# Rotary half-swap moved from DMAs to TensorE, and compression weights moved into the streaming weight ring, in a two-layer decoder trunk

## The reference, cut to what matters

```python
def apply_rope(x, cos, sin):
    half = HEAD_DIM // 2
    x1, x2 = xf[..., :half], xf[..., half:]
    return jnp.concatenate([x1 * cos - x2 * sin, x2 * cos + x1 * sin], axis=-1)

def compress_blocks(k, w1, w2, pe):            # 63 blocks of 32 tokens, stride 16
    flat = (k[:, idx] + pe).reshape(B, nc, N_KV, CMP_L * HEAD_DIM)
    return jax.nn.silu(flat @ w1) @ w2         # w1: 2048 x 256

q = apply_rope(q, cos, sin)                    # 8 heads of 64
kc, k_s, k_w = (apply_rope(t, cos, sin) for t in (kc, k_s, k_w))
y_attn = nsa_mixer(q, kc, vc, k_s, v_s, k_w, v_w, nsa_g, cmp_k_w1, ...)
```

## Time and profile before

| | us |
|---|---|
| median of three executions | 3422.77 |
| the profiled execution | 3423.22 |
| its span, first to last instruction | 3421.5 |
| PE busy | 3256.8 (95%) |
| POOL busy | 1281.6 (37%) |
| DVE busy | 1588.4 (46%) |
| mean granted TensorE clock, share of full speed | 0.977 |

### The profile page before, as it was taken

How to read it: one execution, slowest core, us unless ns; L and a number is a source line. 1 busy time by engine, 2 the same in 40 slices (tenths; PEclk the granted TensorE clock), 3 DMA queues, 4 the chain that set the end, 5 groups by cost and what they waited for, 6 DMA issues and landing times.

```text
span 3421.5 us, 38488 instructions
## 1 busy us (share of the span) xinstructions
PE 3256.8 (95%) x15485; PEld 2654.5 (78%) x15485; DVE 1588.4 (46%) x1998; ACT 771.8 (23%) x1274; POOL 1281.6 (37%) x1271
## 2 busy tenths in 40 slices
PE   5999998998999999999999999989979999999999
PEld 4888886676778888888878888867658788888887
DVE  6643245887537443232365333568754432222223
ACT  2100114666212000000010001256651210000002
POOL 2433332333434444444424334223334344444442
PEclk7999999999899999999999999999999999999999
DMA  6434620000512221111133355200014111111111
GB/s 228 134 102 135 189 77 25 1 1 1 197 43 87 74 69 55 50 50 50 50 125 99 111 160 153 50 13 1 1 64 153 38 49 50 50 50 50 50 45 61
DMA packets 281881, 255.66 MB, mean 75 GB/s; under 512 B 10091, under 2 KB 262247, under 8 KB 281192
## 3 DMA queue, kind: packets, MB, share of 16 engines
q1 hardware_dynamic: 266866, 199.27, 19.7%
q10 hardware_dynamic: 14838, 53.94, 4.1%
HBM read 215.42 MB, written 30.41 MB: 72 GB/s over the span
## 4 chain that ended last, share of the span: by engine, by line
PE 88%; DVE 7%; ACT 2%; issue 2%; POOL 0%; ACTq 0%; POOLq 0%; DVEq 0%
PE lin L917 76%; PE aux L1093 2%; DVE pTL L1637 2%; PE pv L1107 2%; DVE negm L1631 1%; PE pv L1108 1%; PE lin L1069 1%; PE lin L1070 1%; PE pv L957 1%; PE lin L1048 1%; ACT pTH L1340 1%; DVE acc L711 1%; ACT prob L1324 0%; DVE tmp L1657 0%; PE lin L1072 0%
## 5 line engine op out<-in xcount | busy, mean ns | idle before, releaser
L890 POOL TENSOR_SCALAR whi<-wraw 128x512 fp32r<-128x512 f32 x476 | 386.5, 812 | 1589.6 <-PE lin L917 1565.8
L917 PE MATMUL lin<-hH,whi 128*128 128x512 f32 x2272 | 708.0, 393 | 15.4 <-DVE hL L521 12.6
L892 POOL TENSOR_TENSOR wlo<-wraw,whi 128x512 fp32r<-128x512 f32 x476 | 706.9, 1485 | 39.7
L917 PE MATMUL lin<-hL,whi 128*128 128x512 f32 x2272 | 703.4, 391 | 0.0
L917 PE MATMUL lin<-hH,wlo 128*128 128x512 f32 x2272 | 702.2, 390 | 0.0
L917 PEld LDWEIGHTS lin<-hH,whi 128*128 128x128 f32 x2272 | 425.1, 189 | 107.7 <-issue 22.0
L917 PEld LDWEIGHTS lin<-hL,whi 128*128 128x128 f32 x2272 | 428.6, 189 | 90.2
L917 PEld LDWEIGHTS lin<-hH,wlo 128*128 128x128 f32 x2272 | 428.3, 188 | 90.3
L1686 DVE SCALAR_TENSOR_TENSOR xT<-lin,adac,xT 128x1024 f32<-128x1024 f32 x144 | 184.8, 1283 | 567.0 <-PE lin L917 567.0
L870 POOL TENSOR_SCALAR prob<-prob,fac 128x640 f32<-128x640 f32 (+7 forms) x256 | 184.5, 721 | 466.8 <-DVE fac L1621 448.9
L1706 DVE TENSOR_TENSOR tmp<-tmp 128x1024 f32<-128x1024 f32 x64 | 138.4, 2162 | 440.0 <-ACT tmp L1386 439.9
(11 more groups left out here) (236 smaller groups left out, 3681.9 us busy)
## 6 DMA issues: line engine op xcount, KB each, us to landing
wraw<-in_w_ff SPq DMA_DIRECT2D x128, 512.0 KB, 3.9
wraw<-in_w_ada SPq DMA_DIRECT2D x80, 512.0 KB, 3.8
wraw<-in_w_in SPq DMA_DIRECT2D x78, 512.0 KB, 5.0
adar<-in_w_ada SPq DMA_DIRECT2D x16, 512.0 KB, 11.4
x_keep<-xT ACTq DMA_DIRECT2D x4, 2048.0 KB, 9.1
mix_keep<-tmp ACTq DMA_DIRECT2D x16, 512.0 KB, 3.5
gate_keep<-ropes ACTq DMA_DIRECT2D x16, 512.0 KB, 6.6
wraw<-in_w_o SPq DMA_DIRECT2D x16, 512.0 KB, 3.9
```

What stands on the lines that cost most here:

```text
L890: pool.tensor_scalar(high, raw, 1.0, 1.0, ALU.mult, ALU.mult).then_inc(w_hi, 1)
L892: pool.tensor_tensor(wlo[:, SLOT[n], hf], raw, high.bitcast(F32), ALU.subtract).then_inc(w_split, 1)
L917: mm = pe.matmul(lin[c % 2][:, hf], w, m(k)[:, hf], start=first, stop=last)
```

## The change

Three things change together. The half-swap becomes a matmul: `rot`, a 128x128 matrix of 0, 1 and -1 made by POOL at the start, is multiplied with `fbuf` into the PSUM tensor `aux`, two matmuls of 512 columns with 32-bit operands, and DVE multiplies `aux` with the sine table. `sgn`, the rotate DMAs and their buffers go. The compression weights become tiles of the ring: four tiles between the loads of q2 and q3, and four between q3 and ks. A tile of them is two DMAs and frees its slot when PE has used it (`cmp_used`). PE does each rotation one projection later than the one it belongs to.

```diff
-        for name, off in (("q3", O_Q + 3 * P), ("ks", O_KS), ("vs", O_VS), ("kw", O_KW), ("ns", O_NSA), ("vw", O_VW)):
+        tiles += [("cmp", layer, 0, t) for t in range(CMP_T)]
+        dense("w_in", 0, O_Q + 3 * P, ["q3"])
+        tiles += [("cmp", layer, 1, t) for t in range(CMP_T)]
+        for name, off in (("ks", O_KS), ("vs", O_VS), ("kw", O_KW), ("ns", O_NSA), ("vw", O_VW)):
...
-    _count[_s] += 16
+    _count[_s] += 32 if _t[0] == "cmp" else 16
...
+            if t[0] == "cmp":
+                src = a["cmp_v_w1" if t[2] else "cmp_k_w1"]
+                for lh in range(2):
+                    r0 = (lh * CMP_L // 2 + t[3] * LPT) * HD
+                    sp.dma_start(wraw[64 * lh:64 * lh + 64, s, :].rearrange("p (k n) -> p k n", k=LPT),
+                                 src[layer, r0:r0 + LPT * HD, :].rearrange("(k p) n -> p k n", p=HD)).then_inc(raw_in[s], 16)
+                return
...
-            AUXED = ["vs", "nsaT", "vw"]
-            ROTATED_AFTER = {"q3": ["kc"], "vs": ["q0"], "kw": ["q1"], "ns": ["q2"], "vw": ["q3", "ks", "kw"]}
+            AUXED = ["kc", "q0", "q1", "q2", "q3", "ks", "vs", "kw", "nsaT", "vw"]
...
-                            sp.wait_ge(ada_used, KIND_NO[o] + 1)
+                            sp.wait_ge(dict(ada=ada_used, cmp=cmp_used)[TILES[o][0]], KIND_NO[o] + 1)
...
-                    for name in ROTATED_AFTER.get(TILES[n][6][0], ()) if TILES[n][0] == "split" else ():
-                        rotate(sp, name)
-                    for j, name in enumerate(CMP_BESIDE):
-                        if n == TILE_OF[layer, name]:
-                            load_compression(sp, j // CMP_T, j % CMP_T)
...
+                def rotate(name):
+
+                    aux_begin(name)
+                    pe.wait_ge(z_made, Z.index(name) + 1)
+                    for hf in half:
+                        mm = pe.matmul(aux[:, hf], rot[:, :], fbuf[:, Z.index(name) % 2, hf], start=True, stop=True)
+                    mm.then_inc(aux_done, 1)
...
-                    pe.wait_ge(cmp_w_in[kv], 32 * CMP_T * (layer + 1))
                     for t in range(CMP_T):
+                        n = TILE_OF[("cmp", layer, kv, t)]
+                        pe.wait_ge(raw_in[SLOT[n]], IN_SLOT[n])
...
-                                mm = pe.matmul(pv[:, hc, 0:2 * NC], (cmp_k1, cmp_v1)[kv][:, t, at:at + P], blk[:, l, 0:2 * NC],
+                                mm = pe.matmul(pv[:, hc, 0:2 * NC], wraw[:, SLOT[n], at:at + P], blk[:, l, 0:2 * NC],
                                                start=l == 0, stop=l == CMP_L // 2 - 1)
-                    mm.then_inc(cmp_used, 1)
+                        mm.then_inc(cmp_used, 1)
...
                 dense("vc", H, L)
+                rotate("kc")
                 dense("q0", H, L)
                 dense("q1", H, L)
+                rotate("q0")
...
                 dense("q2", H, L)
+                rotate("q1")
...
                 dense("q3", H, L)
+                rotate("q2")
...
                 dense("ks", H, L)
+                rotate("q3")
                 dense("vs", H, L)
+                rotate("ks")
...
                 dense("ns", H, L)
+                rotate("kw")
...
-                    dve.wait_ge(rot_in[i % 2], 64 * (layer * (4 - i % 2) + i // 2 + 1))
-                    then(dve.tensor_tensor(t1, turns_to[i % 2], sinT[:, :], ALU.mult))
+                    dve.wait_ge(aux_done, AUXED.index(name) + 1)
+                    dve.tensor_tensor(t1, aux[:, :], sinT[:, :], ALU.mult).then_inc(aux_free, 1)
```

More of the change, by code:

```diff
@@ L147 @@
         TILE_OF[_t] = _n
-CMP_BESIDE = [("ga", i) for i in range(3, KC)] + ["kc", "vc", "q0"]
 ADA_STREAM = [n for n, t in enumerate(TILES) if t[0] == "ada"]
@@ L281, in trunk @@
             [("xin", [P, NT, D], F32), ("adar0", [P, KC, 2 * 512], F32)])
-        (qS, kwH, kwL, ksH, ksL), (_, cmp_k1, blk, w2, pe_rows, _, rotated, cmp_v1), (cvH, cvL), (mxH, mxL), (hidH, hidL), (nt, crow, _, acc, posr, posf, adar1), (_, rope, rf), (outb,) = region(
+        (qS, kwH, kwL, ksH, ksL), (_, blk, w2, pe_rows), (cvH, cvL), (mxH, mxL), (hidH, hidL), (nt, crow, _, acc, posr, posf, adar1), (_, rope, rf), (outb,) = region(
             "r_m", 2 * KC * SEQ,
             [("qS", [P, NH, SEQ], F32R)] + [(n, [P, NKV, SEQ], F32R) for n in ("kwH", "kwL", "ksH", "ksL")],
-            [("q_first", [P, NH // 2, SEQ], F32), ("cmp_k1", [P, CMP_T, LPT * CMP_H], F32),
-             ("blk", [P, CMP_L // 2, NKV * 64], F32), ("w2", [P, 2, 2, HD], F32), ("pe_rows", [CMP_L, 2 * P], F32),
-             ("below", [P, 512], F32), ("rotated", [P, SEQ], F32), ("cmp_v1", [P, CMP_T, LPT * CMP_H], F32)],
+            [("qS_", [P, NH, SEQ], F32R), ("blk", [P, CMP_L // 2, NKV * 64], F32), ("w2", [P, 2, 2, HD], F32),
+             ("pe_rows", [CMP_L, 2 * P], F32)],
             [("cvH", [P, 4, SEQ], F32R), ("cvL", [P, 4, SEQ], F32R)],
@@ L299, in trunk @@
         ones = sb("ones", [P, P])
-        sgn = sb("sgn", [P, 1])
+        rot = sb("rot", [P, P])
         causal = sb("causal", [P, P], BF16)
@@ L316, in trunk @@
         hsig, hsil = (tmp[:, 0, i * 256:i * 256 + 4 * NC].rearrange("p (i c) -> p i c", i=2) for i in range(2))
-        turns_to = [rotated[:, :], tmp[:, 1, :]]
         low_half = tmp[0:HD, 0, 0:512]
@@ L371, in trunk @@
         raw_in = [sem(f"raw_in{i}") for i in range(RAW)]
-        rot_in = [sem(f"rot_in{i}") for i in range(2)]
-        cmp_w_in = [sem(f"cmp_w{i}_in") for i in range(2)]
         ada_used, ada_mm = sem("ada_used"), sem("ada_mm")
@@ L595, in begin_gpsimd @@
             keep(identb[:, :], ALU.not_equal, [[-1, P]], 0, 1, 1.0)
-            for i in range(4):
-                then(pool.memset(sgn[32 * i:32 * i + 32, :], -1.0 if i % 2 == 0 else 1.0))
-            pool.sem_inc(tab_made, 1)
+            then(pool.memset(rot[:, :], 0.0))
+            rv = rot[:, :].rearrange("p (a i) -> p a i", a=2)
+            keep(rv[:, :, 0:32], ALU.not_equal, [[-64, 2], [-1, 32]], -32, 1, -1.0)
+            keep(rv[:, :, 32:64], ALU.not_equal, [[-64, 2], [-1, 32]], 0, 1, 1.0)
             then(pool.memset(causal[:, :], 0.0))
@@ L680, in rope_scalar @@
             act.wait_ge(p_vec, 5)
-            act.wait_ge(tab_made, 3)
-            act.activation(rope[:, 1, :], rf[:, 0, :], ACT.Sin, scale=sgn[:, 0:1]).then_inc(p_act, 1)
+            act.activation(rope[:, 1, :], rf[:, 0, :], ACT.Sin).then_inc(p_act, 1)
             act.activation(rf[:, 1, :], rf[:, 0, :], ACT.Sin, scale=0.5).then_inc(p_act, 1)
@@ L1249, in silu @@
                 def silu(kv):
-                    act.wait_ge(cmp_used, 2 * layer + kv + 1)
+                    act.wait_ge(cmp_used, CMP_T * (2 * layer + kv + 1))
                     act.activation(hsig[:, :, :], pv[:, :, 0:2 * NC], ACT.Sigmoid).then_inc(hid_sig, 1)
@@ L1470, in rope @@
                     n_dve[0] += 1
-                    dve.wait_ge(rot_in[i % 2], 64 * (layer * (4 - i % 2) + i // 2 + 1))
-                    then(dve.tensor_tensor(t1, turns_to[i % 2], sinT[:, :], ALU.mult))
+                    dve.wait_ge(aux_done, AUXED.index(name) + 1)
+                    dve.tensor_tensor(t1, aux[:, :], sinT[:, :], ALU.mult).then_inc(aux_free, 1)
+                    dve.wait_ge(aux_free, AUXED.index(name) + 1)
+                    dve.wait_ge(dve_step, n_dve[0])
                     if name == "kc":
```

## The result

The changed kernel takes 3471.11 us (median of four, 3469.14 to 3475.29) against 3422.78: a ratio of 1.0142, 95% interval 1.0128 to 1.0155, so 1.4% slower. The forecast was 3467.7, its range 3453 to 3482.

A forecast was written before the change was run, and what follows sets the result against it. PE was taken to set the time in the projections, so work put on it lengthens the kernel: 3423.2 + 28.0 (rotations) + 2 x 2.2 + 2 x 3.7 (ring gaps) + 4.7 (clock) = 3467.7 us, range 3453 to 3482.

The forecast's parts named there:

- Part 4: Sine product from PSUM, kw's late rope, other engines' work: cost nothing, bound 0 to 0.5 us per layer.
- Part 1: Seven rotations per layer on PE, 2.00 us each (bounds 1.85 to 2.05), 28.0 us in all.
- Rival D: Rotations run at the dense pace, 0.45 us each, 6.4 instead of 28, giving 3446; 5%.
- Part 2: Compression weights in the five-slot ring: waits at compression of k, compression of v and ks.
- (a): Compression of k: its fourth tile lands by 5.6 to 7.5, PE asks at 7.5; hidden, cost 0.
- (b): Compression of v: tiles queue behind q3, a gap of 3.65 where 1.42 stood, +2.2 us per layer.
- (c): ks: loaded only when q3 frees its slot, then split by POOL; new gap, +3.7 us per layer.
- Part 3: TensorE's clock: one fall to half clock per layer behind either gap, 4.7 us in all.
- Rival A: The forecast itself, 3459 to 3475, clock falling once to twice per layer or landings varying; 50%.
- B: Clock stays and gaps are at their low ends, giving 3462, or 3456 with cheaper rotations and sooner loads; 20%.
- C: Slow landings and two clock falls per layer, giving 3481; 20%.
- E: Not slower: half clock in the attention stages moves, up to 79 us back, giving 3423 or 3407; 5%.

The follow-up runs named there:

- e5: e3 with each rotation's two matmuls issued twice, same result: 3467.58 us, ratio 1.013.
- e4: The changed kernel with 16 constant matmuls before the compression of v and before ks, results unchanged: 3464.42 us, ratio 1.012.
- e1: The kernel before with only the rotation moved to TensorE, compression weights keeping their own tensors and early loads: 3446.31 us, ratio 1.0068.
- e3: The changed kernel with ring tiles loaded in the order PE uses them: compression of k, q2, compression of v, q3: 3445.67 us, ratio 1.0067.

## Why the prediction was right, step by step

The measured terms are distances between starts in PE's timelines, of the profiled executions; where two numbers stand, they are layer 0 and layer 1.

| term, both layers | forecast | measured | from |
|---|---|---|---|
| rotations on PE | 28.0 | 24.5 | 14 of 1.75; single ones in the trace 1.73, e5 gives 1.69 each |
| gap before the compression of v | 4.4 | 5.2 | last pair of q2 to the compression: 6.96 and 6.93 against 2.61 before, less 1.73 |
| gap before ks | 7.4 | 7.9 | last pair of q3 to ks: 6.82 and 6.82 against 1.15 before, less 1.73 |
| tiles of v arriving slower than PE uses them | 0 | 2.3 | compression of v at full clock: e4's 8.17 and 8.38 against 7.14 before |
| half clock | 4.7 | 7.2 | the changed kernel less e4: compression of v 1.7 and 0.4, from ks to the end 2.7 and 2.4 |
| sum | 44.5 | 47.1 | the two stages are 47.1 longer |

**The bound.** Right: outside the gaps PE set the pace, and e1 (3446 with no ring gap) shows that what is put on PE there is paid in full. Only at the very end of the stage does the changed kernel's chain run over kw's rope instead (part 4).

**Part 1.** The mechanism was right, the size 14% high, and 1.73 lies below the stated bounds of 1.85 to 2.05. The lower bound came from the shown duration of L491 at half clock, 3.78, halved to 1.89; but shown durations overlap what follows, and the rotation is shown with 1.88 too where it costs 1.73. The upper came from L659, which has one contraction row and a distance of 2.00 around it. About 0.1 of that is at its entry (0.55 from the pair ahead, where the rotation has 0.46); what the rest is, is not settled. Rival D (the dense pace, 0.45) is refuted by e5.

**Part 2.** (a) was hidden, as forecast: no wait stands before the compression of k. (b) and (c) came within half a microsecond per layer each, with the releasers that the prediction named. For (b), start of the compression 6.5 us after SP saw the end of q2 (q3's load is issued at 488.40, less 0.2), against 6.3. The step on the later tiles failed: I had them at 271 GB/s and 1.9 us each, where the windows show 228 to 236 GB/s with the DMA share over 1.1, which is 2.2 to 2.3 us for 512 KB, more than the 1.85 that PE needs. For (c), POOL's split of ks in the trace after:

```profile
515.76 5.42 SPq L430 DMA_DIRECT2D wraw<-in_w_in  x5
...
519.60 0.85 POOL L867 TENSOR_SCALAR whi<-wraw 128x512 fp32r<-128x512 f32 x1 [22.38 <-issue]
520.53 1.27 POOL L869 TENSOR_TENSOR wlo<-wraw,whi 128x512 fp32r<-128x512 f32 x1
```

Load at 515.76, split from 519.60, PE at 521.94. With the issue taken 0.2 after the end of q3 as in the prediction, that is 6.4 after it, which is the number forecast; its parts were not, as the load took 3.8 instead of 4.1 and POOL's split 2.2 instead of 2.0.

**Part 3.** Mis-sized: I took one fall per layer, and there were two, in both layers. The rule of the Trainium skill quoted in the prediction (TensorE: Matmul & The Clock Gate, "HAM oscillation") called this rightly: all four gaps, of 3.9 to 4.05 us, were followed by 0.50. That idleness is the cause is shown by e4. The sum by that rule (9.4 in all) would have been 2.2 too high: 2.7 and 2.4 behind ks were near the 2.34 of one fall, but under the half clock in the compression of v lay a wait for tiles, and in layer 1 that fall came late. Rival A allowed for one or two falls.

**Part 4.** Right: DVE's sine product takes 1.22 from PSUM, against 1.21. kw's rope ended 13.8 us after ns, as forecast, and nothing was added behind vw: PE's last wait there is 0.8 as in the earlier trace rows, though it is now put down to DVE's copy of the gates, which the kw rope delays to the same moment. PE's busy time rose by 32.1 us, not 28, since the slow stretches count as busy.

**The rivals.** B (clock stays) is refuted, C was too high in the loads, E did not occur: the attention stages changed by less than 1 us. That the error is only 3.4 us is partly luck: rotations that were too dear by 3.5 stood against a clock too cheap by 2.5, gaps too cheap by 1.3 and a tile pace of 2.3 that was put at nothing. With the rotations right and the rest as it was, the forecast would have been 3464.2, 6.9 too low. The remaining 0.8 is in how the medians lie to the profiled executions.

## What to carry to other kernels

- When tiles of one ring are loaded by one queue in order, list them in the order of use: a tile that waits for a late slot holds back all behind it. The same bytes in the right order made 25 us go (e3 against the changed kernel).
- The rotation's DMAs, for which no engine on the path waited, cost nothing that these runs show; the same permutation as a matmul with 32-bit operands cost its 1.7 us in full on a TensorE that bounds the kernel. Look for who waits before replacing a wait.
- Price a gap on TensorE with the slow stretch behind it, but subtract what that stretch would have waited for anyway; filling the gap with constant work separates the two.

## What the runs showed of the hardware that was not expected

Tiles of 64 partitions by 4 runs of 1 KB arrived at 228 to 236 GB/s while the DMA share stood at 1.13, where the projection tiles (128 partitions by 8 runs of 512 bytes) made 290 GB/s at a share of 1.20: the longer runs were the slower. No run here separates the length of the runs from the number of partitions or from the size of a DMA (256 against 512 KB). And of the changed kernel's two projection stages with the same gaps, one cost 1.5 us more than the other: 1.1 in how much of the compression of v fell on half clock (10.10 us busy in layer 0, 9.01 in layer 1), 0.4 in the slow pairs behind ks. The changed kernel's executions spread over 6.2 us (3469.1 to 3475.3), those of the kernel before over 4.6 in 27 (3420.8 to 3425.4).

```profile
2196.39 9.01 PE L943 MATMUL pv<-blk,wraw 128*128 128x126 f32 x64 [4.02 <-DMA wraw<-in_cmp_v_w]
```
